# State space layer: rotation table and C powers made a pass ahead, one decay buffer, taps used a tick behind their making

## The chip, the cores and the metric

One Trainium2 chip, one of its cores. The core has TensorE (PE) for matmuls, VectorE (DVE), ScalarE (ACT) and GpSimd (POOL) for elementwise work, and SyncE (SP), which issues DMAs. Each engine runs its own program in order and waits on semaphores of the others. The metric is the device time of one execution in microseconds (us), the median of several runs.

## The reference

A stack of layers on 256 tokens of width 2048, all in float32: a state space layer (S5) with a gate, a sparse attention layer, a layer with differential and stick-breaking attention, and an MLP. The change lies in the first:

```python
def s5_mixer(x, w_in, lam_re, lam_im, log_dt, b_re, b_im, c_re, c_im, d_skip, w_glu, b_glu, w_out):
    u, z = jnp.split(x @ w_in, 2, axis=-1)
    ...
    mag = jnp.exp(lr * dt)
    ar = mag * jnp.cos(li * dt)
    ai = mag * jnp.sin(li * dt)
    ...
    bu_r = jnp.einsum('lbgc,gpc->lbgp', ug, bbar_r)
    bu_i = jnp.einsum('lbgc,gpc->lbgp', ug, bbar_i)
    _, _, h_r, h_i = lax.associative_scan(_complex_linear_combine, (..., bu_r, bu_i), axis=0)
    y = (jnp.einsum('gcp,lbgp->lbgc', c_re.astype(f32), h_r)
         - jnp.einsum('gcp,lbgp->lbgc', c_im.astype(f32), h_i))
    y = ... + d_skip * u
    g = jax.nn.gelu(y)
    y = g * jax.nn.sigmoid(g @ w_glu + b_glu)
    return (y * jax.nn.silu(z)) @ w_out
```

There are 64 groups of 16 channels, with 64 complex states each. A state of a group is multiplied by the complex number a = ar + i ai at each token, and the input of the token is added.

## The kernel before

**The stream of slices.** All weights go through one pipeline. SP loads a slice of 256 rows and 512 columns (512 KB) into one of 8 slots (`raw`). ACT rounds it to a high half (`high`, L1157, a ring of 4), DVE makes the low half by subtraction (`low`, L1766), and PE multiplies by both (`tick`, L521). The program is written tick by tick: in tick t PE multiplies slice t, and ACT and DVE prepare slice t + 3 (`LEAD` is 3). Behind that each engine does what its function `beside(t)` lists for tick t. So the table of ticks in the three `beside` functions sets the order of all work here. ACT may write the high half of slice t + 3 only when PE has done slice t - 1. The state space layer's input product has slices 0 to 31 (8 for each quarter of the columns: two for u, then two for z); slices 32 to 39 are the gated product (`GLU_ORDER`), the next are the output product.

**The state space part beside it.** It runs in four passes q = 0 to 3, each for 16 of the 64 groups, six ticks apart. Four tokens are one block (`PH` = 4), so the scan runs over 64 blocks, with the fourth power of a. The magnitude is in the scan's factor (`decay`, from ACT), the angle in a table of cosines and sines (`rotations`, made by DVE). A pass consists of:

- `b_powers` (DVE): B times the powers of a, compact; `b_spread` (ACT) spreads it to 128 columns (`BB`); `b_turn` (PE) transposes it, four banks; `b_copy` (ACT, L1255) copies these.
- `bu` (PE, L673): the block inputs; `bu_copy` (ACT).
- `inputs` (DVE): turns the inputs back by the table; `scan`; `turn_states`: turns the states forward by the same table (`states`, `states_end`).
- `c_powers` (DVE, L1920 to L1922): C times the powers of a, compact, one buffer; `c_powers_spread` (ACT, L1246) spreads it into `CX[q % 2]`.
- `taps` (PE): the contribution of tokens within a block. It forms the tap blocks from B and C (L688); `taps_copy` (ACT, L1277) copies them into `KD`; then PE adds the skip term with diagonals (L696, made by `diagonals` on ACT, L1284) and the products with the tap blocks (L701) to the output bank.
- `y` (PE, L716): the contribution of the states; `gelu` (ACT, L1312), then `y_split` (DVE): high and low half of the gelu, which the gated product reads.

The PSUM banks of the turns, block inputs and tap blocks form a ring of three (`ring`): a bank is written again when ACT has read it, in the order of filling. Each pass fills seven: four for the B turn, two for the block inputs, one for the taps. `diagonals(q + 1)` waits until the tap products of pass q are done (`taps_done`), since PE reads the diagonals and `KD` until then. `z_epilogue` finishes two quarters of z (ACT's tanh, DVE's product) and so frees the accumulator that the gated product writes.

In this kernel the tick of each is: B powers of pass q + 1 and inputs of pass q in tick 12 + 6q, scan in + 2, end of the states in + 3, C powers of pass q + 1 in + 4, its rotation table in + 5. ACT spreads the C powers of passes 1 to 3 in ticks 17, 23 and 29, copies the B turn in 15, 21 and 27. PE's `taps` are in 11, 18, 24 and 30.

Of the kernel before, what the change touches and what calls it, by code (L numbers as in the profile page):

```python
# [12 lines left out]
P = 128  # L13
# [128 lines left out]
def build(nc, ins, out):  # L142
# [74 lines left out]
    DECAY = ssm("decay", [P, 2, QST, NB])  # L217
# [5 lines left out]
    PW = ssm("power_tmp", [P, 2, 3, 2, NST])  # L223
# [283 lines left out]
    def _(pe):  # L507
# [169 lines left out]
        def taps(q):  # L677
# [12 lines left out]
            ins_.then_inc(ring_full, 1)  # L690
            pe.wait_ge(diag_ready, q + 1)
# [29 lines left out]
        def beside(tau):  # L721
# [15 lines left out]
            if tau == 11:  # L737
                taps(0)
            if tau == 15:
                b_turn(1)  # L740
# [20 lines left out]
            if tau == 30:  # L761
                taps(3)

# [380 lines left out]
    def _(act):  # L1144
# [142 lines left out]
        def decay(q):  # L1287

            if q >= 2:
                act.wait_ge(scanned, q - 1)  # L1290
            nc.scalar.activation(DECAY[:, q % 2, :, 1:NB], SP[:, 6, 8 * q:8 * q + 8].unsqueeze(2).to_broadcast([P, QST, NB - 1]),
                                 ACT.Copy).then_inc(decay_ready, 1)
# [21 lines left out]
        def beside(tau):  # L1314
# [21 lines left out]
            if tau == 6:  # L1336
# [5 lines left out]
                decay(1)  # L1342
# [20 lines left out]
            if tau == 13:  # L1363
                b_spread(1)
            if tau == 15:
# [4 lines left out]
            if tau == 17:  # L1370
                c_powers_spread(1)
                gelu(0)
                c_spread(2)
                decay(2)
# [9 lines left out]
            if tau == 23:  # L1384
                c_powers_spread(2)
                gelu(1)
                c_spread(3)
                decay(3)
# [5 lines left out]
            if tau == 27:  # L1394
                b_copy(3)
            if tau == 28:
                bu_copy(3)
            if tau == 29:
                c_powers_spread(3)
                gelu(2)  # L1400
            if tau == 30:
                taps_copy(3)
                z_epilogue(0)
# [350 lines left out]
    def _(v):  # L1754
# [174 lines left out]
        def rotations(q, i):  # L1929
# [10 lines left out]
            TT(RO[:, i, :, :].rearrange("p s (a b) -> p s a b", a=8), m[0], m[1], ALU.add if i else ALU.subtract)  # L1940

        both = [P, 2, QST * NB]
        cos_ = RO[:, 0, :, :].rearrange("p s n -> p (s n)").unsqueeze(1).to_broadcast(both)
        sin_ = RO[:, 1, :, :].rearrange("p s n -> p (s n)").unsqueeze(1).to_broadcast(both)
# [4 lines left out]
        def turn_inputs(q, i):  # L1949

            if i == 0:
# [10 lines left out]
        def scan(q):  # L1962
            v.wait_ge(decay_ready, q + 1)
            for ri in range(2):
                ins_ = V.tensor_tensor_scan(T2[:, ri, :], DECAY[:, q % 2, :, :].rearrange("p s n -> p (s n)"), T1[:, ri, :],
# [6 lines left out]
        def turn_states(q, i):  # L1972

            if i == 0:
# [41 lines left out]
        def beside(tau):  # L2016
# [27 lines left out]
            if tau == 31:  # L2044
                z_epilogue(0)
                y_split(1)
            for q in range(4):
                first = 12 + 6 * q
                if tau == first - 2 and q:
                    c_powers(q, 0)  # L2050
                    c_powers(q, 1)
                if tau == first - 1 and q:
                    rotations(q, 0)
# [788 lines left out]
```

## Time and profile before

| | us |
|---|---|
| median of 3 runs | 2066.36 |
| lowest and highest run | 2063.89, 2066.52 |
| the profiled execution | 2066.16 |
| its span | 2064.4 |
| PE, DVE, ACT busy in the span | 2031.5, 1302.9, 975.1 |

The state space layer with its gate lies in the first 200 us of the span. There PE, DVE and ACT are busy for 24.61, 23.25 and 14.41 us of the 25 us from 125 on. A timeline row gives start and length of a run of like instructions, and in brackets the idle time ahead of it with what ended it. The length of a row includes the tail of its last instruction, so two rows may overlap by 0.1 us or so; the difference of two starts is the time that the work took in the queue.

### The profile page before, as it was taken

Reading aid. Unit: us, or ns where it says so; the run is one execution under the profiler, and the core shown is the slowest. Engines: PE = TensorE matmul, PEld = TensorE weight load, DVE = VectorE, ACT = ScalarE, POOL = GpSimd, SP = SyncE. Lnnn points to the kernel's source line nnn. Section 1 sums busy time; section 2 is a strip of 40 time slices with the busy share of each in tenths; the row PEclk is TensorE's granted clock in tenths of the full one; section 3 lists DMA queues with packets and bytes.
Section 4 is the critical chain, followed back from the end, with each engine's and each line's share of the span. In section 5 each row is a group of like instructions: output and inputs, shape, how many; then the busy total and the mean of one; then the engine's idle time right before and its main releaser. Section 6 shows DMA issues by size and latency. Waiting matters only on the chain.

```text
span 2064.4 us, 31959 instructions
## 1 busy us (share of the span) xinstructions
PE 2031.5 (98%) x12513; PEld 1790.0 (87%) x12513; DVE 1302.9 (63%) x1770; ACT 975.1 (47%) x1414; POOL 82.1 (4%) x84
## 2 busy tenths in 40 slices
PE   8999999999999999999999999999999999999998
PEld 7898898888989898889899898888888888888886
DVE  6799775456666666658666666556546555655555
ACT  5554554344444445446446546544434434434443
POOL 2000042000000000100000001000000000000000
PEclk9999999999999999999999999999999999999999
DMA  9245567545455554755554554566666666566663
GB/s 284 93 132 180 178 206 223 171 139 169 141 164 151 155 162 137 243 173 165 164 166 150 163 154 152 195 185 191 193 190 190 192 194 184 187 199 184 192 192 106
DMA packets 202936, 360.87 MB, mean 175 GB/s; under 512 B 25361, under 2 KB 33905, under 8 KB 202161
## 3 DMA queue, kind: packets, MB, share of 16 engines
q1 hardware_dynamic: 200656, 351.88, 55.2%
q0 software_dynamic: 1664, 5.97, 0.9%
q8 instruction: 99, 1.62, 0.3%
q10 hardware_dynamic: 480, 1.10, 0.1%
q14 instruction: 37, 0.30, 0.0%
HBM read 356.03 MB, written 2.10 MB: 173 GB/s over the span
## 4 chain that ended last, share of the span: by engine, by line
PE 91%; DVE 5%; ACT 2%; issue 2%; DMA 0%; ACTq 0%; POOL 0%; POOLq 0%; DVEq 0%
PE acc L517 36%; PE acc L521 19%; PE banks L517 8%; PE banks L1113 6%; PE acc L1113 6%; PE banks L1116 3%; PE acc L1116 3%; DVE w_high_low L1766 1%; PE acc L607 1%; PE banks L910 1%; PE banks L882 1%; PE acc L548 1%; ACT w_high_low L1157 1%; PE banks L999 1%; PE banks L977 1%
## 5 line engine op out<-in xcount | busy, mean ns | idle before, releaser
L1766 DVE TENSOR_TENSOR w_high_low<-raw,w_high_low 128x1024 fp32r<-128x1024 f32 x648 | 794.6, 1234 | 605.0 <-ACT w_high_low L1157 603.8
L1157 ACT ACTIVATE w_high_low<-raw 128x1024 fp32r<-128x1024 f32 x648 | 682.0, 1059 | 731.9 <-PE acc L517 325.9
L521 PE MATMUL acc<-x_high_low,w_high_low 128*128 128x256 f32 x3648 | 454.4, 285 | 0.7 <-issue 0.7
L521 PEld LDWEIGHTS acc<-x_high_low,w_high_low 128*128 128x128 f32 x3648 | 443.6, 192 | 3.5 <-issue 2.2
L517 PE MATMUL acc<-w_high_low,x_high_low 128*128 128x512 f32 x1728 | 413.9, 396 | 1.1 <-DVE w_high_low L1766 1.1
L517 PEld LDWEIGHTS acc<-w_high_low,x_high_low 128*128 128x128 f32 x1728 | 322.2, 188 | 68.1 <-issue 1.8
L517 PE MATMUL acc<-w_high_low,h_high 128*128 128x512 f32 x1088 | 292.6, 391 | 2.9 <-DVE w_high_low L1766 1.0
L517 PEld LDWEIGHTS acc<-w_high_low,h_high 128*128 128x128 f32 x1088 | 202.7, 188 | 45.9 <-issue 2.0
L517 PE MATMUL acc<-w_high_low,h_low 128*128 128x512 f32 x544 | 167.7, 389 | 0.0
L1113 PE MATMUL acc<-x_high_low,w_high_low 128*128 128x512 f32 x512 | 161.2, 396 | 1.5 <-DVE x_rows L2119 1.1
L1113 PE MATMUL banks<-x_high_low,w_high_low 128*128 128x512 f32 x512 | 160.8, 395 | 0.0
L517 PE MATMUL banks<-w_high_low,h_high 128*128 128x512 f32 x480 | 128.3, 389 | 0.0
L517 PEld LDWEIGHTS acc<-w_high_low,h_low 128*128 128x128 f32 x544 | 102.1, 188 | 21.4
L1116 PEld LDWEIGHTS banks<-x_high_low,w_high_low 128*128 128x128 f32 x512 | 96.2, 188 | 22.7
L1116 PEld LDWEIGHTS acc<-x_high_low,w_high_low 128*128 128x128 f32 x512 | 96.2, 188 | 22.7
L517 PEld LDWEIGHTS banks<-w_high_low,h_high 128*128 128x128 f32 x480 | 90.1, 188 | 18.7
L1116 PE MATMUL acc<-x_high_low,w_high_low 128*128 128x256 f32 x512 | 100.6, 278 | 0.0
L1116 PE MATMUL banks<-x_high_low,w_high_low 128*128 128x256 f32 x512 | 100.6, 278 | 0.0
L1113 PEld LDWEIGHTS acc<-x_high_low,w_high_low 128*128 128x128 f32 x512 | 78.2, 189 | 2.6 <-DVE x_rows L2119 1.3
L1113 PEld LDWEIGHTS banks<-x_high_low,w_high_low 128*128 128x128 f32 x512 | 77.9, 189 | 0.0
L517 PE MATMUL banks<-w_high_low,h_low 128*128 128x512 f32 x240 | 73.9, 389 | 0.0
L517 PEld LDWEIGHTS banks<-w_high_low,h_low 128*128 128x128 f32 x240 | 45.0, 188 | 9.3
(362 smaller groups left out, 1639.1 us busy)
## 6 DMA issues: line engine op xcount, KB each, us to landing
raw<-in_b_w_in SPq DMA_DIRECT2D x128, 512.0 KB, 3.8
raw<-in_w_mlp_in SPq DMA_DIRECT2D x128, 512.0 KB, 3.7
raw<-in_w_mlp_out SPq DMA_DIRECT2D x128, 512.0 KB, 4.6
raw<-in_w_in SPq DMA_DIRECT2D x96, 512.0 KB, 3.8
raw<-in_kv_w SPq DMA_DIRECT2D x48, 512.0 KB, 4.0
raw<-in_a_w_in SPq DMA_DIRECT2D x32, 512.0 KB, 5.9
raw<-in_b_w_out SPq DMA_DIRECT2D x32, 512.0 KB, 4.6
raw<-in_w_out SPq DMA_DIRECT2D x32, 512.0 KB, 4.6
```

The lines of the kernel that those rows point to most:

```text
L517: ins_ = nc.tensor.matmul(PAIRS[pair][:, t, :], xa[:, kt + j, t * P:(t + 1) * P], wa[:, k, j, :], start=first and n == 0, stop=last and n ...
L521: ins_ = nc.tensor.matmul(ACC[pair][:, m // 2, (m % 2) * TOK:(m % 2 + 1) * TOK], wa[:, k, j, m * P:(m + 1) * P], xa[:, kt + j, :], start=f ...
L548: ins_ = nc.tensor.matmul(PAIRS[pair][:, t, :], xa[:, kt, t * P:(t + 1) * P], wa[:, s % SPLIT, j, :], start=start and s == SPLIT and j == ...
L607: ins_ = nc.tensor.matmul(ACC[0][:, m // 2, (m % 2) * TOK:(m % 2 + 1) * TOK], RAW[:, s, j, m * P:(m + 1) * P], XF[kt // 8][:, kt % 8, :], ...
L882: ins_ = nc.tensor.matmul(bank[:, lo:lo + w], QT[:, h, t * P:(t + 1) * P], keys[:, g:g + 1, 0:w].rearrange("p o k -> p (o k)"), start=Fals ...
L910: ins_ = nc.tensor.matmul(BK[3][:, t * P:(t + 1) * P], PTB[:, n % 2, b * P:(b + 1) * P], v[:, k, g * HD:(g + 1) * HD], start=b < 2, stop=b ...
L977: ins_ = nc.tensor.matmul(BK[m][:, lo:lo + w], DQ[:, h, t * P:(t + 1) * P], DK[:, m, h, 0:w], start=False, stop=t == NT - 1, skip_group_ch ...
L999: ins_ = nc.tensor.matmul(BK[3][:, t * P:(t + 1) * P], cols[:, b * P:(b + 1) * P], v[:, k, h * HD:(h + 1) * HD], start=b < 2, stop=b != 1)
L1113: nc.tensor.matmul(both, WH[:, k, j, m * P:(m + 1) * P], XX[:, 2 * s + j, :, :].rearrange("p c t -> p (c t)"), start=s == 0 and j == 0, st ...
L1116: ins_ = nc.tensor.matmul(both[:, 0:TOK], WL[:, k, j, m * P:(m + 1) * P], XH[:, 2 * s + j, :], start=False, stop=s == SLOTS - 1 and j == 1 ...
L1157: nc.scalar.activation(WH[:, s % SPLIT, :, :], RAW[:, s, :, :], ACT.Copy).then_inc(hi_ready, SLOTS + 1 if first_one else 1)
L1766: V.tensor_tensor(WL[:, k, :, :], RAW[:, p % SLOTS, :, :], WH[:, k, :, :].bitcast(F32), ALU.subtract).then_inc(lo_ready, SLOTS + 1 if isin ...
```

## The change

Two buffers hold the rotation table, used in turn (`ROT[q % 2]`); the second lies in a new tile and in that of the power temporaries, whose last use is in tick 5. The decay factor has one buffer, and each `decay(q)` waits for the scan of the pass before. DVE makes the table of pass q + 1 in ticks 11, 16 and 17, 22 and 23, and the C powers of pass q + 1 in tick 13 + 6q, right behind the inputs. ACT spreads the C powers in ticks 14, 20 and 26. In passes 0 to 2 PE's `taps` only forms the tap blocks, and `inside`, one tick later, does the skip term and the tap products. The last pass is one tick earlier on DVE (29, 30, 31); the first z epilogue moves from tick 30 to 27 on ACT and from 31 to 28 on DVE; both splits of the gelu stand at the end of tick 31, behind the end of the last states.

```diff
-    DECAY = ssm("decay", [P, 2, QST, NB])
+    DECAY = ssm("decay", [P, QST, NB])
+    RO_SIN = ssm("rotations_sin1", [P, QST, NB])
...
-    PW = ssm("power_tmp", [P, 2, 3, 2, NST])
+    RO_COS = ssm("rotations_cos1", [P, QST, NB])
+    PW = at("power_tmp", [P, 2, 3, 2, NST], F32, placed["rotations_cos1"])
+    ROT = [(RO[:, 0, :, :], RO[:, 1, :, :]), (RO_COS[:, :, :], RO_SIN[:, :, :])]
...
             ins_.then_inc(ring_full, 1)
+
+        def inside(q):
+
             pe.wait_ge(diag_ready, q + 1)
             if q:
                 pe.wait_ge(gelu_done, q)
...
             if tau == 11:
                 taps(0)
+            if tau in (12, 19, 25):
+                inside((12, 19, 25).index(tau))
...
             if tau == 30:
                 taps(3)
+                inside(3)
...
         def decay(q):
 
-            if q >= 2:
-                act.wait_ge(scanned, q - 1)
-            nc.scalar.activation(DECAY[:, q % 2, :, 1:NB], ...
+            if q:
+                act.wait_ge(scanned, q)
+            nc.scalar.activation(DECAY[:, :, 1:NB], ...
...
                 decay(0)
-                decay(1)
...
+            if tau == 14:
+                c_powers_spread(1)
...
             if tau == 17:
-                c_powers_spread(1)
                 gelu(0)
                 c_spread(2)
-                decay(2)
+                decay(1)
+            if tau == 20:
+                c_powers_spread(2)
...
             if tau == 23:
-                c_powers_spread(2)
                 gelu(1)
                 c_spread(3)
-                decay(3)
+                decay(2)
+            if tau == 26:
+                c_powers_spread(3)
...
             if tau == 27:
                 b_copy(3)
+                z_epilogue(0)
             if tau == 28:
                 bu_copy(3)
+                decay(3)
             if tau == 29:
-                c_powers_spread(3)
                 gelu(2)
             if tau == 30:
                 taps_copy(3)
-                z_epilogue(0)
...
-            if tau == 31:
+            if tau == 28:
                 z_epilogue(0)
-                y_split(1)
+            if tau in (11, 16, 22):
+                rotations((11, 16, 22).index(tau) + 1, 0)
+            if tau in (11, 17, 23):
+                rotations((11, 17, 23).index(tau) + 1, 1)
             for q in range(4):
-                first = 12 + 6 * q
-                if tau == first - 2 and q:
-                    c_powers(q, 0)
-                    c_powers(q, 1)
-                if tau == first - 1 and q:
-                    rotations(q, 0)
-                    rotations(q, 1)
+                first = 12 + 6 * q - (q == 3)
                 if tau == first:
                     if q < 3:
                         b_powers(q + 1, 0)
                         b_powers(q + 1, 1)
                     inputs(q)
-                if tau == first + 2 or (q == 3 and tau == first + 1):
+                if tau == first + 1 and q < 3:
+                    c_powers(q + 1, 0)
+                    c_powers(q + 1, 1)
+                if tau == first + 2 - (q == 3):
                     states(q)
-                if tau == first + 3:
+                if tau == first + 3 - (q == 3):
                     states_end(q)
-            if tau == 30:
+            if tau == 31:
                 y_split(0)
+                y_split(1)
...
         y_split(2)
-        states_end(3)
         low(0)
```

PE in ticks 11 and 12, before: tap blocks, skip term and tap products in a row, then the 24 matmuls of slice 12.

```order
L688 MATMUL banks<-c_powers_91,b_powers 32x96 [waits ring_read,cx_spread,cx_first]
L688 MATMUL banks<-c_powers_91,b_powers 32x96 x15
L696 MATMUL banks<-u_cols,skip_diagonals 128x256 [waits diag_ready]
L696 MATMUL banks<-u_cols,skip_diagonals 128x256
L701 MATMUL banks<-u_cols,tap_blocks 128x192 [waits ring_read]
L701 MATMUL banks<-u_cols,tap_blocks 128x128
L701 MATMUL banks<-u_cols,tap_blocks 128x64
L701 MATMUL banks<-u_cols,tap_blocks 128x192
L701 MATMUL banks<-u_cols,tap_blocks 128x128
L701 MATMUL banks<-u_cols,tap_blocks 128x64
L521 MATMUL acc<-x_high_low,w_high_low 128x256 [waits lo_ready]
```

And after:

```order
L691 MATMUL banks<-c_powers_93,b_powers 32x96 [waits ring_read,cx_spread,cx_first]
L691 MATMUL banks<-c_powers_93,b_powers 32x96 x15
L524 MATMUL acc<-x_high_low,w_high_low 128x256 [waits lo_ready]
L524 MATMUL acc<-x_high_low,w_high_low 128x256 x23
L702 MATMUL banks<-u_cols,skip_diagonals 128x256 [waits diag_ready]
L702 MATMUL banks<-u_cols,skip_diagonals 128x256
L707 MATMUL banks<-u_cols,tap_blocks 128x192 [waits ring_read]
L707 MATMUL banks<-u_cols,tap_blocks 128x128
L707 MATMUL banks<-u_cols,tap_blocks 128x64
L707 MATMUL banks<-u_cols,tap_blocks 128x192
L707 MATMUL banks<-u_cols,tap_blocks 128x128
L707 MATMUL banks<-u_cols,tap_blocks 128x64
```

The 24 matmuls of slice 12 moved in between the tap blocks and the skip term.

ACT from the high half of slice 14 (tick 11) to tick 16, before. `tap_blocks` are the tap copies, `skip_diagonals` the diagonals of pass 1, `b_powers` the spread of the B powers, `b_rows` the copies of the turned B:

```order
L1157 ACTIVATE w_high_low<-raw 128x1024
L1277 ACTIVATE tap_blocks<-banks 32x6x32 x4
L1284 ACTIVATE skip_diagonals<-constants,param_cols 128x128 x2
L1157 ACTIVATE w_high_low<-raw 128x1024 x2
L1238 ACTIVATE b_powers<-b_powers_compact 64x64x16 x2
L1157 ACTIVATE w_high_low<-raw 128x1024 x2
L1255 ACTIVATE b_rows<-banks 128x512 x4
L1157 ACTIVATE w_high_low<-raw 128x1024
L1299 ACTIVATE u_cols<-acc 128x512 x2
```

And after (all line numbers are 9 higher; `c_powers_94` is the spread of the C powers of pass 1):

```order
L1166 ACTIVATE w_high_low<-raw 128x1024
L1286 ACTIVATE tap_blocks<-banks 32x6x32 x4
L1293 ACTIVATE skip_diagonals<-constants,param_cols 128x128 x2
L1166 ACTIVATE w_high_low<-raw 128x1024 x2
L1247 ACTIVATE b_powers<-b_powers_compact 64x64x16 x2
L1166 ACTIVATE w_high_low<-raw 128x1024
L1255 ACTIVATE c_powers_94<-c_powers_compact 64x48x16 x2
L1166 ACTIVATE w_high_low<-raw 128x1024
L1264 ACTIVATE b_rows<-banks 128x512 x4
L1166 ACTIVATE w_high_low<-raw 128x1024
L1308 ACTIVATE u_cols<-acc 128x512 x2
```

The spread of the C powers of pass 1 now stands ahead of slice 18 and of the copies of the turned B; the diagonals kept their place.

DVE in ticks 12 to 14, before: the second operation of the inputs of pass 0, the low half of slice 16, three small operations, slice 17:

```order
L1955 TENSOR_TENSOR products_b<-rotations,block_inputs 128x1024
L1959 TENSOR_TENSOR products_a<-products_a,products_b 128x512
L1960 TENSOR_TENSOR products_a<-products_a,products_b 128x512
L1766 TENSOR_TENSOR w_high_low<-raw,w_high_low 128x1024
L2071 TENSOR_SCALAR param_cols<-param_cols 128x8
L2073 CAST causal_rounded<-constants 128x384
L2074 CAST ident_rounded<-constants 128x128
L1766 TENSOR_TENSOR w_high_low<-raw,w_high_low 128x1024
```

And after; `c_powers_compact` are the C powers of pass 1:

```order
L1967 TENSOR_TENSOR products_b<-rotations,block_inputs 128x1024
L1971 TENSOR_TENSOR products_a<-products_a,products_b 128x512
L1972 TENSOR_TENSOR products_a<-products_a,products_b 128x512
L1778 TENSOR_TENSOR w_high_low<-raw,w_high_low 128x1024
L1932 TENSOR_TENSOR products_b<-a_powers,c_compact 128x384
L1824 TENSOR_TENSOR products_b<-a_powers,c_compact 128x384
L1934 TENSOR_TENSOR c_powers_compact<-products_b 128x3x128
L1932 TENSOR_TENSOR products_b<-a_powers,c_compact 128x384
L1824 TENSOR_TENSOR products_b<-a_powers,c_compact 128x384
L1934 TENSOR_TENSOR c_powers_compact<-products_b 128x3x128
L2085 TENSOR_SCALAR param_cols<-param_cols 128x8
L2087 CAST causal_rounded<-constants 128x384
```

The six operations of the C powers are inserted behind slice 16.

## Rows read from the trace of the kernel before

**Rows 1.** The page: the span and each engine's busy time.

```profile
span 2064.4 us, 31959 instructions
PE 2031.5 (98%) x12513; PEld 1790.0 (87%) x12513; DVE 1302.9 (63%) x1770; ACT 975.1 (47%) x1414; POOL 82.1 (4%) x84
```

**Rows 2.** PE's waits, 0 to 330 us: line, releaser, total us, count, longest.

```profile
PE banks L701 <- ACT tap_blocks L1277: 3.7, 4, 2.5
...
PE banks L696 <- ACT y_cols L1312: 0.5, 1, 0.5
```

**Rows 3.** PE's timeline, 50 to 260 us: start us, length us, line, operands [idle].

```profile
63.33 1.13 PE L696 MATMUL banks<-u_cols,skip_diagonals 128*128 128x256 f32 x4
64.85 1.75 PE L701 MATMUL banks<-u_cols,tap_blocks 128*128 128x192 f32 x12 [0.39 <-ACT tap_blocks L1277]
66.42 11.76 PE L521 MATMUL acc<-x_high_low,w_high_low 128*128 128x256 f32 x96
78.01 1.94 PE L649 MATMUL banks<-constants,b_powers 128*128 128x128 f32 x16
...
82.66 3.68 PE L673 MATMUL banks<-u_phases,b_rows 128*128 128x64 f32 x32
...
89.20 1.97 PE L716 MATMUL banks<-states,c_powers 128*32 128x63 f32 x128
...
99.19 3.25 PE L701 MATMUL banks<-u_cols,tap_blocks 128*128 128x192 f32 x12 [2.48 <-ACT tap_blocks L1277]
...
112.10 1.94 PE L649 MATMUL banks<-constants,b_powers 128*128 128x128 f32 x16
...
140.90 1.95 PE L649 MATMUL banks<-constants,b_powers 128*128 128x128 f32 x16
...
165.26 1.22 PE L521 MATMUL acc<-h_high,w_high_low 128*128 128x256 f32 x8 [1.16 <-DVE z_cols L2004]
```

**Rows 4.** Windows of PE: length, busy us, granted clock, DMA share, GB/s.

```profile
98.00:100.00 2.00, 0.81 (x3) 0.52 0.08 17
104.00:106.00 2.00, 2.00 (x16) 0.78 0.13 29
162.00:168.00 6.00, 4.84 (x41) 1.00 0.27 87
```

**Rows 5.** ACT's timeline, 66 to 97 us.

```profile
66.64 0.70 ACT L1284 ACTIVATE skip_diagonals<-constants,param_cols 128x128 f32<-128x128 f32 x2 [1.84 <-PE banks L701]
...
91.85 1.71 ACT L1246 ACTIVATE c_powers<-c_powers_compact 64x768 f32<-64x768 f32 x2 [3.92 <-DVE c_powers_compact L1922]
93.57 1.28 ACT L1312 ACT_TABLE_LOAD   x1
...
95.49 0.84 ACT L1227 ACTIVATE c_powers<-c_compact 64x256 f32<-64x256 f32 x2
...
96.88 1.04 ACT L1157 ACTIVATE w_high_low<-raw 128x1024 fp32r<-128x1024 f32 x1
```

**Rows 6.** DVE's timeline, 68 to 92 us.

```profile
68.32 1.23 DVE L1766 TENSOR_TENSOR w_high_low<-raw,w_high_low 128x1024 fp32r<-128x1024 f32 x1 [5.64 <-ACT w_high_low L1157]
69.47 0.69 DVE L1900 TENSOR_TENSOR products_b<-b_factors,b_natural 128x512 f32<-128x512 f32 x1
...
73.57 1.23 DVE L1953 TENSOR_TENSOR products_a<-rotations,block_inputs 128x1024 f32<-128x1024 f32 x1
...
77.36 1.23 DVE L1766 TENSOR_TENSOR w_high_low<-raw,w_high_low 128x1024 fp32r<-128x1024 f32 x1
...
80.12 2.33 DVE L1965 TENSOR_TENSOR_SCAN products_b<-decay,products_a 128x512 f32<-128x512 f32 x2
...
83.69 1.22 DVE L1766 TENSOR_TENSOR w_high_low<-raw,w_high_low 128x1024 fp32r<-128x1024 f32 x1
...
88.55 0.55 DVE L1920 TENSOR_TENSOR products_b<-a_powers,c_compact 128x384 f32<-128x384 f32 x1
...
91.85 1.22 DVE L1766 TENSOR_TENSOR w_high_low<-raw,w_high_low 128x1024 fp32r<-128x1024 f32 x1
```

More of the change, by code:

```diff
@@ L1287, in decay @@
         def decay(q):
-            if q >= 2:
-                act.wait_ge(scanned, q - 1)
-            nc.scalar.activation(DECAY[:, q % 2, :, 1:NB], SP[:, 6, 8 * q:8 * q + 8].unsqueeze(2).to_broadcast([P, QST, NB - 1]),
+            if q:
+                act.wait_ge(scanned, q)
+            nc.scalar.activation(DECAY[:, :, 1:NB], SP[:, 6, 8 * q:8 * q + 8].unsqueeze(2).to_broadcast([P, QST, NB - 1]),
                                  ACT.Copy).then_inc(decay_ready, 1)
@@ L1939, in rotations, with turning @@
             TT(m[1], coarse[1], fine[1 - i], ALU.mult)
[L1940 to L1944, printed above, removed]
+            TT(ROT[q % 2][i].rearrange("p s (a b) -> p s a b", a=8), m[0], m[1], ALU.add if i else ALU.subtract)
+        def turning(q):
+            return [x.rearrange("p s n -> p (s n)").unsqueeze(1).to_broadcast([P, 2, QST * NB]) for x in ROT[q % 2]]
         def wide2(x):
@@ L1949, in turn_inputs @@
         def turn_inputs(q, i):
+            cos_, sin_ = turning(q)
             if i == 0:
@@ L1964, in scan @@
             for ri in range(2):
-                ins_ = V.tensor_tensor_scan(T2[:, ri, :], DECAY[:, q % 2, :, :].rearrange("p s n -> p (s n)"), T1[:, ri, :],
+                ins_ = V.tensor_tensor_scan(T2[:, ri, :], DECAY[:, :, :].rearrange("p s n -> p (s n)"), T1[:, ri, :],
                                             0.0, ALU.mult, ALU.add)
@@ L1972, in turn_states @@
         def turn_states(q, i):
+            cos_, sin_ = turning(q)
             if i == 0:
@@ L2724, in _ @@
         GP.memset(KD[:, :, :, :], 0.0).then_inc(zeroed, 1)
-        GP.memset(DECAY[:, :, :, 0:1], 0.0).then_inc(zeroed, 1)
+        GP.memset(DECAY[:, :, 0:1], 0.0).then_inc(zeroed, 1)
         pool.wait_ge(tr_full, TR_X + 8)
```

## The prediction

> **What bounds the kernel now.** I read the page first [rows 1]: TensorE (PE) is busy for 2031.5 us, 98% of the span, so whatever delays PE in the state space layer reaches the end, and a change there can win no more than PE loses there. Then PE's waits and its timeline from 62 to 191 us, for those losses [rows 2, 3]. They are four waits for ACT's tap copies, 3.7 us in all: 2.48 us in pass 1 (ahead of 99.19) and 0.39 in each other pass (64.85 is one). Also in pass 1, 0.5 us for ACT's gelu. And 1.16 us for DVE ahead of the gated product (165.26). The stall of pass 1 costs clock too. The granted clock is 0.52 in 98 to 100 us, 0.78 in 104 to 106 [rows 4]: 1.2 GHz for a time, and then 2.4 GHz again. From the tap products to the next B turn PE takes 112.10 - 99.19 = 12.91 us for three ticks, and in pass 0, at the full clock, 78.01 - 64.85 = 13.16 for four; a tick is 11.76 / 4 = 2.9. So one such drop costs 12.91 - (13.16 - 2.9) = 2.65 us.
>
> Then ACT and DVE for the cause [rows 5, 6]. The stall of pass 1 is ACT's: it waits 3.92 us for DVE's C powers (91.85), loads the gelu's table (1.28 us), and reaches the tap copies late. DVE is the engine to look at. From 68.32 on its work is nearly gapless, and it runs behind PE: it is in tick 13 (slice 16) at 77.36, when PE is already in tick 15. DVE uses up the lead of three slices that it is given. What DVE makes in tick t is there when PE is two to three ticks further.
>
> **The change, part by part.** DVE's blocks, start to start, from [rows 6]: low half of a slice 1.14; B powers 73.57 - 69.47 = 4.10; inputs 77.36 - 73.57 = 3.79; scan with first turn 83.69 - 80.12 = 3.57; end of the states 88.55 - 83.69 less two low halves = 2.58; C powers 91.85 - 88.55 = 3.30.
>
> *Second rotation buffer, one decay buffer.* Count and sizes of the instructions stay. The table for pass 1 moves to tick 11, into the 5.64 us that DVE idles before 68.32: six operations like that at 69.47, about 4.1 us, leave the dense stretch. The decay copies only move; each new wait is for a scan several ticks old. I cost both at nothing; without that idle time as cover the table would cost its 4.1 us.
>
> *Tap products a tick behind.* This removes PE's 0.39 us in passes 0 and 2. But ACT still issues the next diagonals in the tick of the tap copies, and they wait for the tap products (66.64, right behind PE's, which end at 66.4). Queued behind them on ACT is the high half of slice 15, and behind that DVE's low half (68.32). PE now does tick 12 first, from 63.33 (2.9), then the diagonals (1.0 of the 1.13) and the tap products (66.42 - 64.85 = 1.57): they end at 68.8. So ACT's diagonals start at 69.0, and DVE's slice 15 at 70.75 instead of 68.32: **2.4 us late**; the moved table fills only what is idle there anyway.
>
> *C powers a pass ahead.* ACT now spreads the C powers of pass 1 in tick 14, ahead of slice 18 and of the copies of the turned B rows; DVE makes them in tick 13, behind B powers and inputs. DVE: 70.75 + 1.14 + 4.10 + 3.79 + 1.14 + 3.30 = 84.2. ACT: spread 1.70, a high half 0.97, the first B copy 0.5 (a quarter of a turn's), hops of 0.1: 87.5. Who waits is PE: the B turn has four banks in a ring of three, and the fourth is free only with that first copy. Before, it ran at 78.01 + 3 x 0.43 = 79.3. **PE stands still for 8 us: +8.2**, in which the 2.4 above are contained.
>
> *Pass 1 to pass 2.* Now PE, ACT and DVE form one loop instead of running side by side. PE from the fourth bank: 0.43, a tick 2.9, block inputs 3.6, a tick 2.9, outputs 1.97: 11.8. ACT: table load and gelu 95.49 - 93.57 = 1.92, C copy and decay 96.88 - 95.49 = 1.39, high half 0.97: 4.3. DVE: 1.14 + 4.10 + 3.79 + 1.14 + 3.30 = 13.5. ACT: 3.2 as above. Sum 32.8; a restart at 1.2 GHz adds 2.65: 35.5. Before: 112.10 - 78.01 = 34.1. **+1.4.** PE has 28 us of work in it, so it waits some 4.9 us at the fourth bank.
>
> *Pass 2 to pass 3.* The same without the table load: 31.5 + 2.65 = 34.1, against 140.90 - 112.10 = 28.8. **+5.3**, with a stall of about 3.6 us.
>
> *Pass 3 to the gated product.* Its first slice needs the split of pass 0's gelu, which now stands behind all of pass 3's states. Up to DVE's slice 32: bank 0.43, tick 2.9, block inputs 3.6, their copy 0.7, decay 0.6, high half 0.97, hops: 9.4. DVE: three low halves 3.42, inputs 3.79, scan and turn 3.57, end of the states 2.58, the split 1.07: 14.4. Sum 23.8 + 2.65 = 26.5; before 165.26 - (140.90 + 1.29) = 23.1. **+3.4**, with some 2.2 us of waiting where 1.16 was. The earlier z epilogue wins nothing: the queue is late already. From the gated product on, the work follows as before.
>
> Sum: 8.2 + 1.4 + 5.3 + 3.4 = **+18.3 us**. The profiled run took 2066.16 us with a span of 2064.4; the median is 0.2 above it. So I forecast 2066.4 + 18.3 = **2084.7 us**.
>
> On the table load, the row shows 1.28 us, and the gelu and the next copy follow within 1.92 us of its start [rows 5]. The Trainium skill (ScalarE: Activation LUTs, What ACT_TABLE_LOAD costs) gives about 2.66 us for a switch, a drain of 1380 ns included; by an estimate from that page the second loop would grow by 1.4 us, and the time would be 2086.1. The trace shows no such drain and decides.
>
> **What I don't know.** The new restarts: at the low end they cost nothing, if a wait at this place leaves the clock alone (three times 2.65 less: +10.3). Against it: 0.5 and 2.48 us of waiting with one short block between them did lower it, and each new stall is longer than 2.48. I take 2.65 for each. At the high end a longer stall keeps the low level 2.5 us longer, 1.2 us more each: +22. Hops and ring: 1 us either way.
>
> **Rivals.**
> A. *The C powers don't hold ACT up, and the change does what it looks like.* Then the stalls of [rows 2, 3] go: 2.48 + 0.5 + 2 x 0.39 + 1.16, and the drop of 2.65: -7.6, **2058.8 us**. This needs DVE's C powers of pass 1 by 79.3 - 3.2 = 76.1; I count them for 84.2, and even from 68.32 on (no delay by the diagonals) they come at 81.8. For it speaks that DVE has a table less to make in the dense stretch, and that the wait of 3.92 us goes.
> B. *The stalls come, the clock stays.* +10.3: **2076.7**. It decides itself by the granted clock behind each.
> C. *A fourth drop, at the gated product.* +18.3 + 2.65: **2087.3**. Against it: with 1.16 us of waiting there the clock stayed at 1.00 [rows 4]. The Trainium skill (TensorE: Matmul & The Clock Gate, HAM oscillation) tells of a kernel in which every recurring wait of PE is followed by a restart at half rate. By it all four waits here would drop the clock; the trace agrees for the long wait of pass 1 only.
> D. *The loops are shorter than their rows*, since engines hand over earlier than block by block: 1 to 2 us in each of the four parts, +13: **2079.4**.
>
> **How the numbers follow.** Forecast 0.60, C 0.13, D 0.10, B 0.07, A 0.05, and 0.05 for one stall and A's gains that cancel to within 4 us. The range reaches from B to C with longer drops: 2077 to 2091. 0.2% (4.1 us) is about what a measurement of this kernel can tell from no change: faster 0.04, same 0.04, slower 0.92.
>
> **What would show it.** In the trace of the changed kernel: PE waits about 8 us inside the B turn of pass 1, released by ACT's copy into the B rows, and about 5 and 4 us in passes 2 and 3; ACT's spread of the C powers waits for DVE before each; the clock falls behind each. DVE's slice 15 starts at about 70.8. The gated product starts near 184 instead of 165.3. Wrong would be: no wait in the B turn (the ring or the order misread), or the waits but no low clock (B).

## The result, and the profile after

The changed kernel is **slower by 13.7 us**: 2080.12 us in the median of 4 runs (2079.03 to 2081.65), against 2066.44 us for the kernel before in 4 runs beside it. The ratio is 1.007, with a 95% interval of 1.0055 to 1.0084. The forecast was 2084.7 us with a range of 2077 to 2091. The profiled execution took 2081.65 us with a span of 2079.9, 15.5 us more than the span of [rows 1]. The runs of one kernel often lie on two levels some 2.4 us apart, so effects of 2 us or less are read from the traces here, not from the medians; one execution of the last kernel below took 6731.04 us and is left out of its ratio.

The page of the changed kernel, which answers to [rows 1]:

```profile
span 2079.9 us, 31961 instructions
...
PE 2034.4 (98%) x12513; PEld 1793.4 (86%) x12513; DVE 1303.1 (63%) x1770; ACT 975.0 (47%) x1414; POOL 82.7 (4%) x84
```

PE is busy for 2034.4 us where it was busy for 2031.5. So some 3 of the 15.5 us are matmuls that took longer, at the lower clock, and the other 12.5 are idle. PE's waits in the same stretch as [rows 2] (line, releaser, total us, times, longest us):

```profile
PE banks L652 <- ACT b_rows L1264: 15.1, 3, 8.0
...
PE acc L524 <- issue: 2.2, 2, 1.9
```

The three waits of 15.1 us for ACT's copy into the B rows did not exist before. PE's timeline (start us, length us, line, operands, [idle before, and its releaser]) shows where they are. It answers to [rows 3]:

```profile
77.60 1.53 PE L652 MATMUL banks<-constants,b_powers 128*128 128x128 f32 x12 [0.52 <-ACT b_powers L1247]
87.11 1.12 PE L652 MATMUL banks<-constants,b_powers 128*128 128x128 f32 x4 [7.98 <-ACT b_rows L1264]
...
98.47 1.97 PE L722 MATMUL banks<-states,c_powers 128*32 128x63 f32 x128
...
120.47 0.66 PE L652 MATMUL banks<-constants,b_powers 128*128 128x128 f32 x4 [3.58 <-ACT b_rows L1264]
...
153.85 0.66 PE L652 MATMUL banks<-constants,b_powers 128*128 128x128 f32 x4 [3.57 <-ACT b_rows L1264]
...
165.24 1.97 PE L722 MATMUL banks<-states,c_powers 128*32 128x63 f32 x128
...
179.13 2.03 PE L524 MATMUL acc<-h_high,w_high_low 128*128 128x256 f32 x8 [1.88 <-issue]
...
209.29 1.17 PE L520 MATMUL acc<-w_high_low,h_high 128*128 128x512 f32 x4 [0.55 <-DVE w_high_low L1778]
```

The reader is to take two things from it. The B turn, one row of 16 matmuls at 78.01, 112.10 and 140.90 before, is cut into 12 and 4 in each pass: the fourth bank comes only after 7.98, 3.58 and 3.57 us of idling. And behind pass 3 everything is displaced together: the gated product starts at 179.13 where it started at 165.26. The last row is the first wait in the product behind it. Before, that one was here (PE's timeline of the kernel before):

```profile
193.94 1.17 PE L517 MATMUL acc<-w_high_low,h_high 128*128 128x512 f32 x4 [0.50 <-DVE w_high_low L1766]
```

With the fourth bank of the kernel before at 78.01 + 1.29 = 79.30, 113.39 and 142.19 (three quarters of the B turn, as the forecast had it), the path of PE divides as follows:

| stretch | before, us | after, us | difference | forecast |
|---|---|---|---|---|
| start to bank 4 of pass 1 | 79.30 | 87.11 | +7.8 | +8.2 |
| bank 4 of pass 1 to bank 4 of pass 2 | 34.09 | 33.36 | -0.7 | +1.4 |
| to bank 4 of pass 3 | 28.80 | 33.38 | +4.6 | +5.3 |
| to the gated product | 23.07 | 25.28 | +2.2 | +3.4 |
| gated product to the first wait behind it | 28.68 | 30.16 | +1.5 | 0 |
| sum | | | +15.4 | +18.3 |

The rest of the program adds 0.1 us. Who holds PE up shows in ACT's timeline, which answers to [rows 5] (same columns):

```profile
68.43 0.70 ACT L1293 ACTIVATE skip_diagonals<-constants,param_cols 128x128 f32<-128x128 f32 x2 [4.06 <-PE banks L707]
...
83.66 1.70 ACT L1255 ACTIVATE c_powers<-c_powers_compact 64x768 f32<-64x768 f32 x2 [5.02 <-DVE c_powers_compact L1934]
...
86.46 1.57 ACT L1264 ACTIVATE b_rows<-banks 128x512 f32<-128x512 f32 x3
...
97.22 1.28 ACT L1321 ACT_TABLE_LOAD   x1
100.51 0.60 ACT L1321 ACTIVATE y_cols<-banks 128x512 f32<-128x512 f32 x1 [2.01 <-PE banks L722]
```

and in DVE's, which answers to [rows 6]:

```profile
70.18 1.23 DVE L1778 TENSOR_TENSOR w_high_low<-raw,w_high_low 128x1024 fp32r<-128x1024 f32 x1 [3.94 <-ACT w_high_low L1166]
...
83.06 0.56 DVE L1934 TENSOR_TENSOR c_powers_compact<-products_b 128x384 f32<-128x384 f32 x1
```

In order of time: the diagonals wait 4.06 us for the tap products (68.43), and behind them slice 15 reaches DVE at 70.18. DVE finishes the C powers at 83.06 + 0.56. ACT has waited 5.02 us for just that (83.66), spreads them, makes a high half, and copies the first bank of B rows at 86.46. That frees PE's fourth bank: 87.11.

Windows of PE (stretch: length, busy us and matmuls, granted clock, share of DMA, GB/s), against [rows 4]:

```profile
84.00:88.00 4.00, 0.89 (x5) 0.50 0.33 108
91.00:92.00 1.00, 1.00 (x12) 1.00 0.59 174
121.00:124.00 3.00, 3.00 (x17) 0.52 1.04 380
124.00:125.00 1.00, 1.00 (x9) 0.73 1.04 338
179.00:182.00 3.00, 2.87 (x13) 0.52 0.00 0
```

The granted clock of 0.50 is the level of 1.2 GHz, 1.00 that of 2.4 GHz. The clock is at 1.2 GHz inside and behind the stall of pass 1, at full speed again from 91, at 1.2 GHz from 121 to 124 behind the second, and once more from 179 to 182 behind the wait of 1.88 us ahead of the gated product. Behind the third stall it falls too: the windows from 156 to 158 show 0.50.

### The profile page after: what moved, and what is told of

Its sections match the earlier page's. It is cut to its first block, busy times and chain, and to the rows that moved or that the text cites. A ratio compares the mean times of both kernels' runs of the same rounds, so it can differ in the third digit from the quotient of the medians.

```text
span 2079.9 us, 31961 instructions
## 1 busy us (share of the span) xinstructions
PE 2034.4 (98%) x12513; PEld 1793.4 (86%) x12513; DVE 1303.1 (63%) x1770; ACT 975.0 (47%) x1414; POOL 82.7 (4%) x84
## 4 chain that ended last, share of the span: by engine, by line
PE 92%; DVE 4%; ACT 2%; issue 2%; DMA 0%; ACTq 0%; POOL 0%; POOLq 0%; DVEq 0%
PE acc L520 36%; PE acc L524 20%; PE banks L520 8%; PE banks L1122 6%; PE acc L1122 6%; PE banks L1125 3%; PE acc L1125 3%; PE acc L610 1%; PE banks L919 1%; PE banks L891 1%; DVE w_high_low L1778 1%; ACT w_high_low L1166 1%; PE acc L551 1%; PE banks L676 1%; PE banks L1008 1%
```

## The experiments

Theory: ACT stands at the spread of the C powers, which DVE makes late, and PE's ring of three banks passes that on; the diagonals that still wait for the later tap products put 2 to 3 us more in front of it; the low clock behind each stall adds the rest. Rivals: another wait of the B turn (its powers, the ring, a DMA) with the C powers as bystander; the loops themselves as the cause, with no cost of the clock; and a cost of the later tap products alone.

**The spread back in its old place.** ACT issues the spread of the C powers ahead of the gelu again, as before; DVE's order and the tap products stay as changed.

```diff
             if tau == 13:
                 b_spread(1)
-            if tau == 14:
-                c_powers_spread(1)
...
             if tau == 17:
+                c_powers_spread(1)
                 gelu(0)
```

(the same for 20/23 and 26/29; the first z epilogue moves to 29 on ACT, behind the last spread and a wait for it, and to 30 on DVE, since it writes over what the spread reads).

> The changed kernel, but ACT spreads the C powers of passes 1 to 3 in ticks 17, 23 and 29 again, ahead of the gelu (DVE still makes them in 13, 19 and 25); the first z epilogue comes after the last spread (29 on ACT, 30 on DVE), since it writes over their source. Theory 1 (ACT, held at the spread until DVE's C powers are done, keeps the B copies from PE): the waits of 8.0, 3.6 and 3.6 us ahead of the fourth bank of the B turns vanish, but for some 1 us in pass 1; 2 to 3 us appear at the outputs of pass 0 and ahead of the gated product. 12 us less than the changed kernel: 2068, with 1 us either way. Rival (DVE's longer queue, not the place of ACT's spread, is what PE waits for): the waits move elsewhere and the time stays within 4 us of 2080.

Measured: 2069.73 us (10 runs), ratio 1.0017 (1.0008 to 1.0027), span 2068.1: 11.8 us less than the changed kernel, where 12 was expected. The median is 0.7 us above the upper end of the expected 2067 to 2069. PE's timeline of this kernel:

```profile
81.27 0.66 PE L652 MATMUL banks<-constants,b_powers 128*128 128x128 f32 x4 [1.12 <-ACT b_rows L1264]
...
93.62 1.97 PE L722 MATMUL banks<-states,c_powers 128*32 128x63 f32 x128 [2.37 <-DVE states L1996]
...
167.18 2.05 PE L524 MATMUL acc<-h_high,w_high_low 128*128 128x256 f32 x8 [4.94 <-issue]
```

The wait of 7.98 us is 1.12, those of passes 2 and 3 are gone. So the place of the spreads on ACT, with the z epilogue that goes with it, is worth 11.8 of the 15.5 us, although DVE still makes the C powers as in the changed kernel. The rivals that blame another wait in the B turn fall. What is left is 2.37 us ahead of the outputs of pass 0, for DVE's states, and 4.94 ahead of the gated product.

**The diagonals behind the tap products.** Only the diagonals of passes 1 to 3 move, one tick later on ACT.

```diff
                 taps_copy(0)
+            if tau == 12:
                 diagonals(1)
```

(the same for 18/19 and 24/25).

> The changed kernel, but ACT makes the next pass's diagonals one tick later (12, 19, 25 instead of 11, 18, 24), behind the next high half. Theory 1: ACT no longer holds back slices 15, 22 and 28; DVE's slice 15 starts at 68 instead of 70.2 us, the wait at the fourth bank of pass 1 shrinks from 8.0 to about 4.5 us, and the two later ones stay at 3.6. 4 us less in all: 2076. Rival (the diagonals' wait is idle time that costs nothing): 2080, the wait at 8.0 us.

Measured: 2078.36 us (4 runs), ratio 1.0057 (1.004 to 1.0074), span 2077.2. DVE's and PE's timeline of this kernel:

```profile
67.29 1.23 DVE L1779 TENSOR_TENSOR w_high_low<-raw,w_high_low 128x1024 fp32r<-128x1024 f32 x1
```

```profile
84.21 1.12 PE L652 MATMUL banks<-constants,b_powers 128*128 128x128 f32 x4 [4.82 <-ACT b_rows L1264]
...
177.94 1.19 PE L524 MATMUL acc<-h_high,w_high_low 128*128 128x256 f32 x8 [1.89 <-issue]
...
206.61 1.15 PE L520 MATMUL acc<-w_high_low,h_high 128*128 128x512 f32 x4 [0.54 <-DVE w_high_low L1779]
```

Slice 15 reaches DVE at 67.29, with no idle ahead of it, instead of 70.18, and the stall falls from 7.98 to 4.82 us. PE entered this stretch 1.0 us later in this run (63.07 against 62.07), so the gain at the fourth bank is 3.9 us from that point on. DVE's gain from that point is 70.18 - 67.29 + 1.0, the same 3.9: the delay by the diagonals passes through to PE in full. The span is 2.7 us below that of the changed kernel, where 4 was expected: 2.9 at the fourth bank, less 0.7 and 1.0 because the clock stayed low longer in passes 1 and 3, plus 1.5 because it did not fall at the gated product. The window of the longer drop in pass 3:

```profile
152.00:157.00 5.00, 5.00 (x25) 0.50 0.37 117
```

**Both edits together.**

> Both edits: the spread of the C powers back in ticks 17, 23, 29, and the diagonals one tick later. What is left of the change is the second rotation table, DVE's earlier C powers, the taps a tick behind, and the order at the end. Theory 1: no wait of PE over 1 us until the gated product, which waits about 5 us for DVE's split of the first gelu, behind the states of pass 3; 17 us less than the changed kernel, 2063, or 3 us less than the kernel before. Rival: DVE's order costs by itself, and the time stays above the kernel before (2066.4).

Measured: 2065.59 us (10 runs), ratio 0.9999 (0.999 to 1.0009), span 2063.7. From the B turn of pass 1 to the gated product its PE timeline holds only the first two of these waits and the 0.39 us of pass 3's tap products:

```profile
89.30 1.97 PE L722 MATMUL banks<-states,c_powers 128*32 128x63 f32 x128 [0.52 <-DVE states L1997]
...
162.86 2.05 PE L524 MATMUL acc<-h_high,w_high_low 128*128 128x256 f32 x8 [4.93 <-issue]
...
193.21 1.17 PE L520 MATMUL acc<-w_high_low,h_high 128*128 128x512 f32 x4 [0.52 <-DVE w_high_low L1777]
```

The B turns run through, the clock is 1.00 from 77 to 98 us, and the loss of 15.5 us is gone. The place of the spreads and that of the diagonals carry it. The two overlap: the spans put the edit of the spreads at 11.8 us alone and 13.5 on top of that of the diagonals, and the edit of the diagonals at 2.7 alone and 4.4 on top of that of the spreads. The other parts (second rotation buffer, one decay buffer, C powers a pass ahead on DVE, tap products a tick behind, the new order of the last pass) neither cost nor win anything when taken together; they were not tried one by one. The time is 2.6 us above the expected 2063: the wait ahead of the gated product has grown from 1.16 to 4.93, and the clock falls there, so that the stretch up to the next wait takes 193.21 - 162.86 = 30.35 us instead of 28.68.

**The splits of the gelu first in the last pass.** As both, and DVE splits the gelu of pass 0 ahead of pass 3's states instead of behind them.

```diff
                 if tau == first + 2 - (q == 3):
+                    if q == 3:
+                        y_split(0)
                     states(q)
                 if tau == first + 3 - (q == 3):
+                    if q == 3:
+                        y_split(1)
                     states_end(q)
-            if tau == 31:
-                y_split(0)
-                y_split(1)
```

> As the kernel with both edits, and in the last pass DVE splits the gelu of pass 0 ahead of the scan (tick 30) and that of pass 1 ahead of the end of the states (tick 31). Theory 1: the wait of 5 us ahead of the gated product goes, and with it a drop of the clock; under 1 us each ahead of its next two slices. 2058, 8 us less than the kernel before. Rival (the outputs of pass 3 then wait for their states as long as was won): 2063, as with both edits alone.

Measured: **2060.95 us** (6 runs), ratio 0.9972 (0.996 to 0.9985), span 2059.7. PE's timeline of this kernel:

```profile
160.93 1.21 PE L524 MATMUL acc<-h_high,w_high_low 128*128 128x256 f32 x8 [0.49 <-DVE g_low L1805]
...
164.59 1.21 PE L524 MATMUL acc<-h_high,w_high_low 128*128 128x256 f32 x8 [0.53 <-DVE g_low L1805]
...
187.50 1.17 PE L520 MATMUL acc<-w_high_low,h_high 128*128 128x512 f32 x4 [0.51 <-DVE w_high_low L1777]
```

Two waits of half a microsecond stand where 4.93 stood, and the first wait behind comes at 187.50, against 193.21 in the kernel with both edits and 193.94 before. The time is 3 us above the expected 2058; a drop of the clock behind this layer, shown in the last section, takes 1.5 of them. The same kernel again:

> The kernel with both edits and the splits first, run once more in more rounds beside the kernel before: 2061, 5 us less than before. A second look at whether its gain holds; with no gain it would be 2066.

Measured: 2060.81 us (8 runs), ratio 0.9971 (0.9961 to 0.9982). This version beats the kernel before by 5.7 us and the changed one by 19.

**The splits first alone**: the same edit, in the changed kernel.

> The changed kernel with one edit: in the last pass DVE splits the gelu of pass 0 ahead of the scan (tick 30) and that of pass 1 ahead of the end of the states (tick 31). Theory 1 (the last wait is for the split that stands behind all states, and 1.88 us of waiting there can drop the clock): no wait ahead of the gated product, the clock stays at 1.00 there; 1.9 + 1.5 us less, 2076.7; the three waits in the B turns stay. Rival (the gated product then waits for something else as long): 2080.

Measured: 2079.13 us (4 runs), ratio 1.0061 (1.0046 to 1.0077), span 2078.6, where 2076.7 was expected. From the outputs of pass 2 to the first wait behind the gated product PE takes 208.17 - 167.73 = 40.44 us, against 209.29 - 165.24 = 44.05 in the changed kernel: the 3.6 us are there. But PE entered the stretch 1.1 us later, and with the same stalls the clock stayed low for longer stretches of PE's work. From the fourth bank of pass 1 to the outputs it is 100.04 - 88.20 = 11.84 us against 98.47 - 87.11 = 11.36. The windows of this kernel:

```profile
88.00:91.00 3.00, 2.80 (x13) 0.50 0.47 152
...
155.00:160.00 5.00, 4.57 (x22) 0.50 0.37 120
```

From the fourth bank of pass 3 it is 167.73 - 155.43 = 12.30 against 11.39. So 2.5 of the 3.6 us are taken back, 1.1 by the later entry and 1.4 by the two longer low stretches. The edit does its work; its result is clouded by the stalls left in place.

**PE kept busy in the stalls.** The changed kernel, with matmuls of 512 columns into an accumulator that is free then, ahead of the fourth bank: 34 in pass 1, 15 in pass 2, none in pass 3. They compute nothing that is used.

```diff
             for n in range(4):
+                if n == 3 and q in (1, 2):
+                    for i in range(34 if q == 1 else 15):
+                        nc.tensor.matmul(ACC[q - 1][:, i % 2, :], XH[:, 0, 0:P], ...)
                 bank = ring(b_fill(q, n))
```

> The changed kernel, and PE does matmuls of 512 columns into a free accumulator while it waits ahead of the fourth bank of the B turn: 34 in pass 1 (about 7.4 us of its 8.0) and 15 in pass 2 (3.3 of 3.6). They add work without a result and change nothing else; pass 3 is left alone. Theory 1 (a stall costs its length and then a stretch at 1.2 GHz): the waits' ends stay where they are, the granted clock stays at 1.00 behind them, and each saves the 1.5 us that PE loses there now: 3 us, 2077. Rival (the low clock costs nothing here, since ACT and DVE set the pace of the loop): 2080, with the clock at 1.00 too.

Measured: 2078.96 us (4 runs), ratio 1.0057 (1.004 to 1.0074), span 2077.1. Its PE timeline, and its windows:

```profile
88.06 0.66 PE L656 MATMUL banks<-constants,b_powers 128*128 128x128 f32 x4 [0.26 <-ACT b_rows L1268]
...
119.97 0.66 PE L656 MATMUL banks<-constants,b_powers 128*128 128x128 f32 x4 [0.17 <-ACT b_rows L1268]
...
151.86 1.12 PE L656 MATMUL banks<-constants,b_powers 128*128 128x128 f32 x4 [3.58 <-ACT b_rows L1268]
```

```profile
88.00:92.00 4.00, 3.94 (x34) 1.00 0.29 98
120.00:124.00 4.00, 4.00 (x35) 1.00 0.97 314
156.00:157.00 1.00, 1.00 (x6) 0.50 1.00 377
```

The fourth bank of pass 1 comes when it came in the changed kernel (88.06, with PE 0.93 us later into the stretch: 87.13), so what PE does inside the stall doesn't change its end. But from bank to bank it is 31.91 and 31.89 us instead of 33.36 and 33.38. **A restart at 1.2 GHz costs 1.45 and 1.49 us here**, not the 2.65 of the forecast. In pass 3, where the stall is left as it was, the clock is 0.50 up to 157. The span is 2.8 us less than that of the changed kernel, close to the 3 expected, but in part by luck: besides the 2.9 us of the two restarts PE came 0.95 us later to the fourth bank of pass 1 and lost 0.85 more in pass 3, and gained 1.5 at the gated product, where the clock stayed up. The median is only 1.2 us less.

**The same in the kernel before**: ten such matmuls in pass 1, between the skip term and the tap products.

> The kernel before, and PE does 10 such matmuls (2.2 us) between the skip term and the tap products of pass 1, where it waits 2.48 us. Theory 1: the clock stays at 1.00 from 98 to 105 us; of the 2.65 us that this gives, about 0.5 are lost to a longer wait ahead of the gated product: 2064.2. Rival (DVE sets the end of this stage): the gated product starts at 165.3 as before, and the time is 2066.3.

Measured: 2063.89 us (10 runs), ratio 0.9989 (0.9979 to 0.9999), span 2063.8. PE's timeline of this kernel:

```profile
99.28 1.75 PE L705 MATMUL banks<-u_cols,tap_blocks 128*128 128x192 f32 x12 [0.20 <-ACT tap_blocks L1281]
...
109.55 1.94 PE L649 MATMUL banks<-constants,b_powers 128*128 128x128 f32 x16
...
163.19 1.21 PE L521 MATMUL acc<-h_high,w_high_low 128*128 128x256 f32 x8 [1.65 <-DVE z_cols L2008]
```

In [rows 3] the tap products start at 99.19 and the next B turn at 112.10: 12.91 us. Here it is 109.55 - 99.28 = 10.27, with the clock at 1.00 from 98 to 106. The 2.64 us are the 2.65 that the forecast worked out. So the price was right where it was read, and wrong where it was carried to. The gated product starts 2.07 us earlier than before, at 163.19 behind a wait of 1.65 us, so the rival by which DVE holds it at 165.3 falls.

**The tap products later in the kernel before**, with the diagonals where they were, and then with the diagonals one tick later as well.

```diff
             ins_.then_inc(ring_full, 1)
+
+        def inside(q):
+
             pe.wait_ge(diag_ready, q + 1)
...
                 taps(0)
+            if tau in (12, 19, 25):
+                inside((12, 19, 25).index(tau))
```

> The kernel before with one part of the change alone: skip term and tap products of passes 0 to 2 one tick behind the tap blocks. ACT's diagonals stay where they are. Theory 1 (the diagonals hold back ACT's next high half, and with it DVE): DVE's slice 15 comes 2.4 us later, PE waits about 0.7 and 1.2 us in the B turn of pass 1 and 4 to 5 us ahead of the gated product; 2068, 1.7 us more than before. Rival (the waits for the tap copies, 3.3 us of 3.7, simply go, and the drop of the clock with them): 2061.

Measured: 2068.24 us (10 runs), ratio 1.0008 (0.9998 to 1.0018), which doesn't tell it from the kernel before, span 2065.3. DVE's timeline of this kernel, then PE's:

```profile
70.01 1.23 DVE L1772 TENSOR_TENSOR w_high_low<-raw,w_high_low 128x1024 fp32r<-128x1024 f32 x1 [7.85 <-ACT w_high_low L1163]
```

```profile
80.09 0.66 PE L649 MATMUL banks<-constants,b_powers 128*128 128x128 f32 x4 [1.12 <-ACT b_rows L1261]
...
164.77 1.67 PE L521 MATMUL acc<-h_high,w_high_low 128*128 128x256 f32 x8 [4.37 <-DVE z_cols L2010]
```

> The kernel before with skip term and tap products one tick behind, and ACT's diagonals one tick later too. C powers, tables and the last pass as before. Theory 1: no wait over 0.6 us from 63 us to the gated product, no drop of the clock in pass 1, 3 to 4 us of waiting ahead of the gated product (for DVE's z epilogue) and a drop of the clock there: 2063, 3 us less than before. Rival (the early C powers and the second table are needed for any gain): 2066.

Measured: 2063.89 us (10 runs), ratio 0.9991 (0.9981 to 1.0001), again not clear of no change, span 2062.1. PE's timeline and a window of this kernel:

```profile
161.50 2.07 PE L521 MATMUL acc<-h_high,w_high_low 128*128 128x256 f32 x8 [3.85 <-DVE z_cols L2011]
...
191.52 1.17 PE L517 MATMUL acc<-w_high_low,h_high 128*128 128x512 f32 x4 [0.53 <-DVE w_high_low L1773]
```

```profile
63.00:160.00 97.00, 94.26 (x1204) 1.00 0.37 124
```

With the diagonals in place the later tap products hold slice 15 back from 68.32 to 70.01, as they do in the changed kernel. (Counted from the products of the tap powers, at 61.96 here and 62.49 before, that is 2.2 us; the forecast had 2.4.) With the diagonals behind them it is there at 66.76, PE's timeline has no wait from 63 to 150 us, and the clock is 1.00 throughout; the gated product starts 3.76 us earlier than in [rows 3], but now behind a wait of 3.85 us that drops the clock, so that 191.52 is only 2.42 us ahead of 193.94. In the kernel with both edits, which has these two and the rest of the change, that wait comes at 193.21: the rest of the change costs 1.7 us on top of them. So moving the tap products, with the diagonals behind them, is the part that wins by the trace; the full gain of 5.7 us was only measured with the rest of the change and the earlier splits, and these splits were not tried without the rest.

## Why the forecast was right in kind and 4.6 us too high

**The hold-up of ACT: right.** Forecast and measured: slice 15 on DVE at 70.75 and 70.18; C powers done at 84.2 and 83.6; bank 4 at 87.5 and 87.11; the stall 8 and 7.98. The spread and diagonal runs confirm the two causes and their order of size.

**The loops: the blocks right, two prices wrong.** The stalls were forecast at 4.9, 3.6 and 2.2 us and came at 3.58, 3.57 and 1.88. Without restarts the loops were forecast at 32.8 and 31.5 and measure 31.91 and 31.89 in the kept-busy run.

- *The gelu's table load* stood as 1.28 us on the path of the loop from pass 1 to 2. ACT's timeline shows it at 97.22, and the gelu at 100.51 behind 2.01 us of waiting for PE's outputs: ACT loaded the table while PE still worked. In [rows 5] the load follows ACT's previous work at once and the gelu follows the load; there it was on ACT's path because ACT was late, not because it must be. ACT's timeline of the kernel before has the gelu here, with no idle time ahead of it:

  ```profile
  94.87 0.60 ACT L1312 ACTIVATE y_cols<-banks 128x512 f32<-128x512 f32 x1
  ```

  This step failed by 1.28 us, and it makes the forecast's stall of 4.9 us the same 3.6 as in pass 2.
- *The restart* was carried from the stall of the kernel before at 2.65 each. It is 1.45 to 1.49 by the kept-busy run: three times 1.2 us too much, 3.6 us. This is the mis-sized term that carries most of the miss. In part it is luck: the same kind of restart costs 2.5 us in pass 3 of the diagonal run, so the forecast's price lies within what neighbouring kernels show. The high end of the range had a longer stall keep the low level 2.5 us longer, at 1.2 us more. No row shows that term. Behind the stall of 7.98 us the clock was low from about 83.6 to 90.4, 3.4 us longer than in passes 2 and 3, but PE idled through that part and the restart cost no more than theirs.
- In the other direction, the blocks of each of the two loops summed to 0.4 us too little (31.9 against 31.5, the table load left out).

**The clock at the gated product: wrong.** The forecast held that a wait of about 2 us there leaves the clock alone and put the drop aside as a rival at 0.13. It came: the stretch behind the wait takes 30.16 us, against 28.68 before. The diagonal run waits 1.89 us at the same place, and the kept-busy run 1.88, both keep the full clock, and take 206.61 - 177.94 = 28.67 and 206.64 - 177.99 = 28.65. So the length of the wait alone doesn't decide, and the drop costs 1.5 us.

**The sum.** +18.3, less 1.3 for the table, less 3.6 for three restarts, plus 1.5 for the fourth, plus 0.8 for the blocks of the two loops, less 0.4 because PE entered the stretch earlier (the products of the tap powers at 62.07 instead of 62.49), gives 15.3, against 15.4 in the table. The medians differ by 13.7, not 15.5: the profiled execution of the changed kernel was the slowest of its four, and its median falls between two pairs of runs. Lowest run against lowest, the difference is 2079.03 - 2063.89 = 15.1. So of the 4.6 us that the forecast was too high, 3 are its terms and the rest is where the median fell.

**The cited rules.** By the Trainium skill (ScalarE: Activation LUTs, What ACT_TABLE_LOAD costs) a switch costs about 2.66 us with its drain, which as an estimate would have added 1.4 us to the second loop. The measurement went the other way: the load shows 1.28 us, the gelu of the kernel before starts right at its end (93.57 + 1.28 = 94.85, and 94.87), and in the changed kernel the load ran in ACT's idle time. The waits in the kernel of the Trainium skill (TensorE: Matmul & The Clock Gate, HAM oscillation) last some 3 to 5 us, and each is followed by a restart at half rate. The three waits in the B turns here, of 7.98, 3.58 and 3.57 us, agree with it. The fourth, of 1.88 us, is shorter than those, so the forecast read too much into the section when it counted it in; here it dropped the clock, and at 1.89 and 1.88 us in the diagonal and the kept-busy run it did not.

**The rivals.** A is excluded by the stalls. B is excluded by the windows. C's mechanism happened, at 1.5 instead of 2.65. D's time of 2079.4 us is near by chance: it had each of the four parts 1 to 2 us shorter than its rows. Without the restarts the second part is 0.9 us shorter (31.91 against 32.8, the table load that overlaps), the third 0.4 longer (31.89 against 31.5), and the fourth, 25.28 less the 1.5 of its restart, is the 23.8 of the forecast. What was shorter were the restarts.

## What to carry to other kernels

Where one engine makes operands and a second spreads them, work that is put a pass ahead must stay behind what the third engine needs next: an early place in an in-order queue is an early wait, and here it cost 11.8 us for three blocks of 1.7 us each. When a product is moved a tick back, move everything that waits for its buffers too (here the diagonals), and look for the next late step (here the split behind the last states) in the same go; together with the spreads in their old place they turned +0.7% into -0.3%. Price a restart of the clock from several rows, and as a range: here stalls of like length cost from 1.5 to 2.5 us.

## What the runs showed of the hardware

The same stall costs different amounts. Behind 3.58 us in the B turn of pass 2 the clock was low from about 121.1 to 124.5 in the changed kernel (0.52 from 121 to 124, 0.73 in the next microsecond), 1.5 us lost; in the diagonal run in pass 3, after 3.58 us too, it was low from about 150.5 to 157.3, and the stretch to the next outputs took 12.40 us instead of 9.90, 2.5 lost. The low stretches of this layer last from 3.4 us to 10.2 us (from about 82.3 to 92.6 in pass 1 of the kernel with the splits first alone), and the ones of 6.8 us and more all start while PE is still idle. The rows show it without a window: the fourth bank's four matmuls take 0.66 us where the clock falls behind them, and 1.12 where it has fallen already.

Nor does a wait of a given length always drop the clock. At the gated product 1.16, 1.65 and 1.88 to 1.89 us kept it in four kernels, 1.88 dropped it in the changed one, and 3.85 to 4.94 dropped it in four. And where nothing was changed, it can fall: behind four waits of 0.69, 1.03, 1.02 and 1.11 us, far past the layer, the next 24 matmuls take 5.72 us in the kernel with both edits and 7.24 in the one with the splits first (7.23 in its second profile):

```profile
325.37 5.72 PE L520 MATMUL acc<-w_high_low,x_high_low 128*128 128x512 f32 x24 [1.11 <-DVE w_high_low L1777]
```

```profile
319.69 7.24 PE L520 MATMUL acc<-w_high_low,x_high_low 128*128 128x512 f32 x24 [1.11 <-DVE w_high_low L1777]
```

The granted clock from 320 to 323 us is 0.50 in the second. In the kernel before with PE kept busy they take 7.09, against 5.73 in the kernel before, so that of the 2.07 us which it was ahead only 0.6 are left in its span. This is why the version that beats both has lost 1.5 of the 6.4 us that it was ahead at 187.50. What decides it stays open: each profile shows one execution, and no run varied the starting point of a stall on its own.
